# A three-block network on one core: modulation rows move from TensorE to VectorE, MLP units take both halves of x in one matmul, and attention probabilities become the stationary operand

## The chip, the core and the metric

The kernel runs on one core of a Trainium2 chip. Its engines have instruction streams of their own and meet only at semaphores: TensorE (PE in the profile, with its weight loads as PEld), VectorE (DVE), ScalarE (ACT), GpSimd (POOL, which only fills a few constants here) and SyncE (SP), which issues the transfers of the weights. The metric is the time of one execution in microseconds. The median of the runs before is 1037.1 us.

## What is computed

Batch 1, 256 tokens, width 1024, all in 32-bit floats. The reference is a first block of two layers and a second block of one layer:

```python
for i in range(DEPTH):                      # 0: gated delta rule, 1: HGRN
    s = conv_gdn_mixer(...) if i % 2 == 0 else hgrn2_mixer(...)
    x = layer_norm(DEEPNORM_ALPHA * x + s, ln_g[i], ln_b[i])
    gate = sigmoid(x @ w_pl_gate[i])
    x = x + (p[i] @ w_pl[i]) * gate
...
mod = silu(c) @ w_ada[l] + b_ada[l]         # c is one row: 1 x 1024 by 1024 x 6144
sh1, sc1, g1, sh2, sc2, g2 = split(mod[:, None, :], 6, axis=-1)
hn = rms(x, norm1_g) * (1 + sc1) + sh1
y = mixer(hn, w_in, ...)                    # 6 forget-gate heads, 4 mLSTM, 6 block-sparse
x = x + g1 * (y @ w_out)
hn = rms(x, norm2_g) * (1 + sc2) + sh2
gate, up = split(hn @ w_gate_up, 2, axis=-1)
x = x + g2 * ((silu(gate) * up) @ w_down)   # inner width 2816
```

In an attention head, `p = softmax(s)` and the output is `p @ v`; in an mLSTM head the scores are divided by `max(|sum|, exp(-m))` instead.

## The kernel before

**Weights.** All large weights come from HBM as 165 slabs, mostly of 1 MB (128 partitions by 2048 numbers), in a fixed order, into a ring of six buffers `RAW`. SyncE issues the load of slab i when the last user of slab i-6 is done (the function `slab`). A matmul operand `w` or `x` is kept as two parts in the format fp32r: a high part H, rounded, and a low part L, the rest. A product is then three matmuls, H·H, H·L and L·H (`products`). For a weight slab, ScalarE writes the high part `WH` (a ring of three, `s_split`) and VectorE subtracts it from the raw slab, in place, as `WL`. For x the parts are `XTH` and `XTL`, for the input of an output projection `YH` and `YL`.

**Steps and order.** The work is cut into named steps. A step such as `ff:7` has a part on each engine that takes part in it (on "TSV": TensorE, then ScalarE, then VectorE). The order in which each engine runs its steps is written out by hand, in the tables `ORDER_T`, `ORDER_S` and `ORDER_V`; an engine never leaves its order. `split:k:i` is the split of slab i. PSUM has eight banks. Those that a step needs are claimed: TensorE waits until the readers of the previous step in that bank are done. Banks 4 to 7 are a ring for the weight units.

**Modulation rows.** `silu(c)` lies as one column per block of 128 inputs in `SCZ`, padded with zeros to 32 columns. The 6144 outputs are 12 rows of 512; each takes two slabs and two steps, `ada:i:0` and `ada:i:1`. These slabs are not split. A step is four matmuls with a 32-column weight, one per quarter of the partitions of one PSUM bank (`t_ada`). ScalarE copies the bank to `MROW` (`s_ada`), and `adat:i` (`t_adat`, `v_adat`) brings the row where it is used: for eight rows by four transposes and a sum over groups on VectorE, for the four gain rows by a matmul with ones.

**Around them.** The tail of each layer of the first block has the layer norm on VectorE (`lna`, `lnb`), transposes of x (`xt`), and the gate product, whose input the VectorE part of `xt` makes. The rows 0, 1 and 2 stand in the first tail, 3 in the last group of the HGRN layer, 8, 6, 7, 9 and 4 in and behind the second tail, 5 in the attention, 10 and 11 between the output projection (`out2`) and the MLP (`ff`).

**Attention.** For head h: `score` (TensorE; VectorE adds the bias and takes a minimum, ScalarE takes the exponential and the sum), `ratio` (VectorE: reciprocal, then it multiplies the 384 probabilities of each partition by it), `turn` (three transposes, a ScalarE copy to `PTT`), `pv` (three matmuls with v stationary, so that the result is already transposed), and for every second head the split of the result to `YH` and `YL`.

**MLP.** `ff:j`, j from 0 to 21, makes 128 gate and 128 up features in one bank: 16 pairs of a block k and a half a, each with three matmuls of 256 columns. ScalarE takes Silu of the gate half, VectorE multiplies, and splits the result. `down` follows.

Of the kernel before, what the change touches and what calls it, by code (L numbers as in the profile page):

```python
# [115 lines left out]
def plan(stage):  # L116
# [351 lines left out]
    end_row()  # L468
    for j in range(FF):
        unit("ff", j, on="TSV", slab=("ff", j), halves=False)  # L470
# [12 lines left out]
gu:0:3:1 ah:0:1 gx:0:3:1 first:ac:0:1 gp:0:4:1 gp:0:4:0 gx:0:3:0 ac:0:1 gu:0:4:1 gu:0:4:0 first:az:0:1 gx:0:4:0 az:0:1
gp:0:5:1 gp:0:5:0 gx:0:4:1 first:ab:0:1 gu:0:5:0 gu:0:5:1 ab:0:1 gx:0:5:0 gp:0:6:0 gp:0:6:1 gx:0:5:1 first:ah:1:0
gu:0:6:0 gu:0:6:1 ah:1:0 gv:0:0 first:ac:1:0 gs:0 first:az:1:0 gks:0 az:1:0 gv:0:1 ac:1:0 go:0 first:ab:1:0 gr:0:0
ab:1:0 gc:1 first:zb:1:0 zb:1:0 first:zb:1:1 norm:q:1 zb:1:1 first:ah:1:1 ah:1:1 gk:1 vtr:1 first:ac:1:1 gkk:1 ac:1:1
first:ab:1:1 gp:1:0:0 first:az:1:1 gp:1:0:1 gu:1:0:0 az:1:1 ab:1:1 gp:1:1:0 gu:1:0:1 out:0:0:0 gu:1:1:0 gp:1:1:1
# [5 lines left out]
first:gate:0:1:0 first:gate:0:1:1 xt:1:0 gate:0:1:0 gate:0:1:1 adat:1 xt:1:1 ada:2:0 ada:2:1 xt:1:2 xt:1:3 first:f:0:0
first:f:0:1 f:0:1 adat:2 f:0:0 first:q1:0:0 q1:0:0 first:q1:0:1 q1:0:1 first:i:0:0 hd:0 i:0:0 hm:0:0 first:i:0:1
hm:0:1 i:0:1 first:f:1:1 first:f:1:0 hm:0:2 first:z1:0:0 hm:0:3 f:1:0 f:1:1 z1:0:0 first:z1:0:1 z1:0:1 hm:0:4
first:q1:1:0 hm:0:5 q1:1:0 hm:0:6 first:q1:1:1 hc:0 q1:1:1 ho:0 first:i:1:0 hd:1 hr:0:0 i:1:0 first:f:2:0 first:i:1:1
f:2:0 hm:1:0 i:1:1 hm:1:1 first:f:2:1 f:2:1 hm:1:2 first:z1:1:1 first:z1:1:0 hm:1:3 z1:1:0 hm:1:4 first:q1:2:0 z1:1:1
hm:1:5 q1:2:0 hm:1:6 first:q1:2:1 hc:1 q1:2:1 ho:1 first:i:2:0 hd:2 hr:1:0 first:i:2:1 i:2:0 first:f:3:0 f:3:0 hm:2:0
i:2:1 hm:2:1 first:f:3:1 f:3:1 first:z1:2:0 hm:2:2 first:z1:2:1 hm:2:3 z1:2:0 hm:2:4 z1:2:1 hm:2:5 first:q1:3:0 hm:2:6
q1:3:0 hc:2 first:q1:3:1 ho:2 q1:3:1 hr:2:0 hd:3 first:i:3:0 i:3:0 first:i:3:1 hm:3:0 first:z1:3:0 i:3:1 hm:3:1 z1:3:0  # L500
hm:3:2 first:z1:3:1 hm:3:3 z1:3:1 hm:3:4 ada:3:0 ada:3:1 hm:3:5 adat:3 out:1:0:0 hm:3:6 out:1:0:1 hc:3 out:1:1:0 ho:3
out:1:1:1 hr:3:0 out:1:0:2 hr:3:1 pl:1:0 out:1:1:2 first:out:1:0:3 first:out:1:1:3 out:1:0:3 out:1:1:3 pl:1:1 ada:8:0
# [1968 lines left out]
```

## Time and profile before

| | |
|---|---|
| runs | 1037.1 us median of 3 (1036.44 to 1039.84) |
| the profiled execution | 1038.47 us, of which the trace spans 1036.7 |
| TensorE matmul busy | 1016.7 us (98%) |
| TensorE weight load busy | 897.0 us (87%) |
| VectorE busy | 718.1 us (69%) |
| ScalarE busy | 508.8 us (49%) |
| DMA | 181.44 MB, mean 175 GB/s |

All times in a trace are microseconds from the start of the span. Matmuls are pipelined: the duration of one in the trace is longer than its distance to the next, so what one costs in a stream is read from the distance of starts. A wait that a trace names is idle time of the engine before an instruction, with what ended it.

### The profile page before, as it was taken

Reading aid. Unit: us, or ns where it says so; the run is one execution under the profiler, and the core shown is the slowest. Engines: PE = TensorE matmul, PEld = TensorE weight load, DVE = VectorE, ACT = ScalarE, POOL = GpSimd, SP = SyncE. Lnnn points to the kernel's source line nnn. Section 1 sums busy time; section 2 is a strip of 40 time slices with the busy share of each in tenths; the row PEclk is TensorE's granted clock in tenths of the full one; section 3 lists DMA queues with packets and bytes.
Section 4 is the critical chain, followed back from the end, with each engine's and each line's share of the span. In section 5 each row is a group of like instructions: output and inputs, shape, how many; then the busy total and the mean of one; then the engine's idle time right before and its main releaser. Section 6 shows DMA issues by size and latency. Waiting matters only on the chain.

```text
span 1036.7 us, 21071 instructions
## 1 busy us (share of the span) xinstructions
PE 1016.7 (98%) x9120; PEld 897.0 (87%) x9120; DVE 718.1 (69%) x1049; ACT 508.8 (49%) x590; POOL 0.5 (0%) x7
## 2 busy tenths in 40 slices
PE   9999999999999999999999999989998999999998
PEld 7999999999875798989898887669975779999986
DVE  6898946698448656867786856855887775655544
ACT  6764444463253552554555343565767553343331
POOL 0000000000000000000000000000000000000000
PEclk9999999999999999999999999999999999999999
DMA  8454333334227663525343544865523447454541
GB/s 357 164 185 163 123 128 130 135 139 163 83 99 287 258 225 111 202 102 186 123 164 123 188 180 180 341 266 218 201 110 123 152 172 286 162 208 159 192 175 41
DMA packets 26298, 181.44 MB, mean 175 GB/s; under 512 B 3040, under 2 KB 3296, under 8 KB 4960
## 3 DMA queue, kind: packets, MB, share of 16 engines
q1 hardware_dynamic: 25056, 174.66, 45.5%
q10 hardware_dynamic: 1152, 5.45, 1.3%
q8 instruction: 73, 1.20, 0.4%
q14 instruction: 17, 0.14, 0.0%
HBM read 179.04 MB, written 1.05 MB: 174 GB/s over the span
## 4 chain that ended last, share of the span: by engine, by line
PE 91%; DVE 4%; DMA 2%; ACT 2%; issue 1%; POOL 0%; ACTq 0%; POOLq 0%; DVEq 0%
PE PS L916 87%; DMA RAW<-wst 2%; PE PS L1157 1%; PE PS L1079 1%; DVE WL L1814 1%; ACT WH L1386 1%; DVE block L2289 0%; DVE layer_ln L2138 0%; PE PS L1006 0%; DVE block L2274 0%; PE PS L1196 0%; PE PS L1307 0%; ACT block L1694 0%; ACT block L1688 0%; DVE block L2269 0%
## 5 line engine op out<-in xcount | busy, mean ns | idle before, releaser
L1814 DVE TENSOR_TENSOR WL<-RAW,WH 128x2048 fp32r<-128x2048 f32 (+1 forms) x138 | 312.1, 2272 | 137.7 <-ACT WH L1386 137.5
L916 PE MATMUL PS<-XTH,WH 128*128 128x256 f32 x1392 | 404.1, 290 | 0.5 <-issue 0.5
L916 PE MATMUL PS<-XTL,WH 128*128 128x256 f32 x1392 | 394.4, 283 | 0.0
L916 PE MATMUL PS<-XTH,WL 128*128 128x256 f32 x1392 | 394.3, 283 | 0.0
L1386 ACT ACTIVATE WH<-RAW 128x2048 fp32r<-128x2048 f32 x138 | 260.8, 1899 | 236.7 <-PE PS L916 223.9
L916 PEld LDWEIGHTS PS<-XTH,WH 128*128 128x128 f32 x1392 | 267.3, 192 | 4.4 <-issue 2.8
L916 PEld LDWEIGHTS PS<-XTL,WH 128*128 128x128 f32 x1392 | 267.5, 192 | 2.5 <-issue 2.4
L916 PEld LDWEIGHTS PS<-XTH,WL 128*128 128x128 f32 x1392 | 267.4, 192 | 0.0
L916 PE MATMUL PS<-WH,YH 128*128 128x512 f32 x224 | 90.0, 402 | 0.0
L916 PE MATMUL PS<-WH,YL 128*128 128x512 f32 x224 | 87.3, 390 | 0.0
L916 PE MATMUL PS<-WL,YH 128*128 128x512 f32 x224 | 87.2, 389 | 0.0
L916 PE MATMUL PS<-WH,XTH 128*128 128x512 f32 x160 | 65.5, 410 | 2.3 <-ACT MROW L1569 2.1
L916 PE MATMUL PS<-WH,XTL 128*128 128x512 f32 x160 | 62.5, 391 | 0.0
L916 PE MATMUL PS<-WL,XTH 128*128 128x512 f32 x160 | 62.4, 390 | 0.0
L916 PEld LDWEIGHTS PS<-WH,YH 128*128 128x128 f32 x224 | 42.1, 188 | 9.6 <-issue 1.1
L916 PEld LDWEIGHTS PS<-WL,YH 128*128 128x128 f32 x224 | 42.1, 188 | 9.3 <-issue 1.0
L916 PEld LDWEIGHTS PS<-WH,YL 128*128 128x128 f32 x224 | 42.0, 188 | 9.0
L916 PEld LDWEIGHTS PS<-layer 128*32 128x32 f32 (+2 forms) x1920 | 39.2, 119 | 9.0 <-issue 4.2
L1736 ACT ACT_TABLE_LOAD x36 | 46.2, 1283 | 0.6
L916 PE MATMUL PS<-layer 128*32 128x16 f32 (+3 forms) x1920 | 43.9, 198 | 0.9 <-DVE layer L2132 0.8
L916 PEld LDWEIGHTS PS<-WH,XTH 128*128 128x128 f32 x160 | 30.1, 188 | 9.9 <-ACT MROW L1569 2.5
L916 PEld LDWEIGHTS PS<-WH,XTL 128*128 128x128 f32 x160 | 30.0, 188 | 6.6
(293 smaller groups left out, 1082.4 us busy)
## 6 DMA issues: line engine op xcount, KB each, us to landing
RAW<-wst SPq DMA_DIRECT2D x162, 1024.0 KB, 4.9
LNW<-lnrow ACTq DMA_DIRECT2D x3, 1024.0 KB, 7.9
RAW<-wst SPq DMA_DIRECT2D x4, 512.0 KB, 5.7
layer<-xt SPq DMA_DIRECT2D x2, 512.0 KB, 5.3
XR<-x ACTq DMA_DIRECT2D x1, 1024.0 KB, 6.8
out<-X SPq DMA_DIRECT2D x4, 256.0 KB, 2.3
CST<-cst ACTq DMA_DIRECT2D x1, 640.0 KB, 8.7
PT<-pt SPq DMA_DIRECT2D x1, 512.0 KB, 5.5
```

Source lines behind the costliest of these rows:

```text
L916: return pe.matmul(o, lhsT, rhs, start=start, stop=stop)
L1079: last = pe.transpose(PS[:, 2 + c, h * P:(h + 1) * P], U[:, c * HG + h, :], ident)
L1157: last = pe.transpose(PS[:, step.banks[0], o:o + P], src[:, c, k * P:(k + 1) * P], ident)
L1386: fn(WH[:, k % SPLIT_RING, 0:n], RAW[:, i % RAW_RING, 0:n], ACT.Copy).then_inc(scalar_done, 1)
L1736: act.preload_act_table_set(wanted)
L1814: tt(WL[:, i % RAW_RING, 0:n], RAW[:, i % RAW_RING, 0:n], as_float(WH[:, k % SPLIT_RING, 0:n]), ALU.subtract).then_inc(vector_done, 1)
```

## The change

Three edits, and a new order for all engines.

1. `ada:i:0` and `ada:i:1` go to VectorE. `v_ada` multiplies each of the eight blocks of a row by its column of `SCZ` and adds it to `MROW`, with one tensor_scalar and seven scalar_tensor_tensor instructions of 512 elements per row; all 128 partial sums stay apart. `t_adat` then sums over the partitions: for the eight rows by four matmuls with the block of `MROW` stationary and 16 columns of ones moving, for the gain rows as before. `s_ada` is gone. A slab of such a row is free when VectorE is done with it.
2. `XTH` and `XTL` become halves of one tile `XHL`, so that `t_ff` can move 512 columns (both halves) past the high weight, and 256 (the high one) past the low weight: 16 pairs, each with one matmul of 512 and one of 256 columns. A unit now fills two banks, with a part to be added: ScalarE copies one (`fl`), VectorE adds (`fs`), and then the rest follows as before from SBUF. With four banks in the ring, two units fit instead of four.
3. In `pv` the transposed probabilities are stationary (128 columns) and v moves (64 columns). `turn` no longer waits for `ratio`; that only takes the reciprocal. The division comes later, on the output of two heads (`ys`), which is then transposed back by two transposes (`yt`) and split.

```diff
@@ def ada(i): def halves():
-            unit("ada", i, 0, on="T", slab=("ada", i, 0), readers="", halves=False)
-            banks = script[-1].banks
+            step("ada", i, 0, on="V", slab=(("ada", i, 0),), readers="")
             end_row()
-            step("ada", i, 1, on="TS", banks=banks, slab=(("ada", i, 1),), opens=False)
+            step("ada", i, 1, on="V", slab=(("ada", i, 1),), readers="")
@@
-                step("pv", n - 2, on="T", banks=(3,))
...
+            step("pv", n - 2, on="T", banks=(3,), opens=n % 2 == 0)
+            if n % 2:
+                t = (n - 2) // 2
+                step("ys", t, on="V")
+                step("yt", t, on="TS" if FOX // 2 <= t < (FOX + ML) // 2 else "TSV", banks=(3,), opens=False)
@@
-        unit("ff", j, on="TSV", slab=("ff", j), halves=False)
+        step("ff", j, on="TSV", banks=(bank(), bank()), slab=[("ff", j)], readers="V", read_in=("fs", j))
+        step("fl", j, on="S")
+        step("fs", j, on="V")
@@ ORDER_V (one line of each)
-first:out:0:0:3 first:out:0:1:3 lna:0:0 lnb:0:0:0 out:0:0:3 out:0:1:3 lna:0:1 lnb:0:0:1 lnb:0:1:0 lnb:0:1:1 xt:0:0:0
+gr:1:1 ada:0:0 ada:0:1 first:out:0:1:3 first:out:0:0:3 out:0:0:3 lna:0:0 out:0:1:3 lnb:0:0:0 lna:0:1 lnb:0:0:1
@@ t_adat
                 for j in range(4):
-                    last = pe.transpose(PS[:, step.banks[0], j * P:(j + 1) * P], MROW[:, j * P:(j + 1) * P], ident)
+                    last = mm(PS[:, step.banks[0], 16 * j:16 * (j + 1)], row[:, j * P:(j + 1) * P], ONES[:, 0:16],
+                              start=j == 0, stop=j == 3)
@@ t_pv
-                mm(o[:, 0:P], V2[:, 0, vcol:vcol + HD], pt[:, 0:P])
...
+                mm(o[:, 0:HD], pt[:, 0:P], V2[:, 0, vcol:vcol + HD])
+                mm(o[:, HD:P], pt[:, P:2 * P], V2[:, 0, vcol:vcol + HD], stop=False)
+                mm(o[:, HD:P], pt[:, 2 * P:3 * P], V2[:, 1, vcol:vcol + HD], start=False).then_inc(tensor_done, 1)
@@ t_ff
-                features(step, xt_part(5)).then_inc(tensor_done, 1)
+                for k in range(KC):
...
+                    for a in range(2):
+                        s, o = slice(a * P, (a + 1) * P), PS[:, step.banks[a], :]
+                        mm(o, wh[:, k, s], XHL[:, k, :, :].rearrange("p e t -> p (e t)"), start=k == 0, stop=False)
+                        last = mm(o[:, 0:T], wl[:, k, s], XTH[:, k, :], start=False, stop=k == KC - 1)
@@ new on VectorE
+            def v_ada(i, part):
...
+                for j in range(4):
+                    c = SCZ[:, 4 * part + j, 0:1]
+                    if part == 0 and j == 0:
+                        last = ts(row, w[:, j, :], c, None, ALU.mult)
+                    else:
+                        last = stt(row, w[:, j, :], c, row, ALU.mult, ALU.add)
+                    if j < 3:
+                        link(last)
@@ ScalarE and VectorE in the MLP
+                fn(FL[:, j % 2], PS[:, b:b + 2, T:2 * T], ACT.Copy).then_inc(scalar_done, 1)
...
+                tt(FT[:, j % 2], PS[:, b:b + 2, 0:T], FL[:, j % 2], ALU.add).then_inc(vector_done, 1)
```

Where the new order puts the rows is best seen in the built programs. VectorE at the start of the first tail, before the change (X<-XR,PS with BN_STATS is `first:out`, the sum of x and the projection; YL is the end of the mixer):

```order
L1825 CAST YH<-layer_x 128x512
L1826 TENSOR_TENSOR YL<-layer_x,YH 128x512
L1997 SCALAR_TENSOR_TENSOR X<-XR_81,PS 128x512
L1998 BN_STATS STAT<-X 128x6
L1997 SCALAR_TENSOR_TENSOR X<-XR_81,PS 128x512
L1998 BN_STATS STAT<-X 128x6
L2010 BN_AGGR AGG<-STAT 128x2
```

And with the change:

```order
L1851 CAST YH<-layer_x 128x512
L1852 TENSOR_TENSOR YL<-layer_x,YH 128x512
L2102 TENSOR_SCALAR MROW<-RAW,SCZ 128x512
L2104 SCALAR_TENSOR_TENSOR MROW<-RAW,SCZ,MROW 128x512 x7
L2026 SCALAR_TENSOR_TENSOR X<-XR_80,PS 128x512
L2029 BN_STATS STAT<-X 128x6
L2026 SCALAR_TENSOR_TENSOR X<-XR_80,PS 128x512
```

A whole row (`ada:0:0` and `ada:0:1`) now stands between the end of the mixer and the first sum of the layer norm. VectorE between the output projection and the MLP, with the change (L2374 ends `out2`, L2209 to L2213 normalize x, L2070 is `xt:5`, the input of the MLP):

```order
L2374 TENSOR_TENSOR X<-X,block_84 128x512
L2102 TENSOR_SCALAR MROW<-RAW,SCZ 128x512
L2104 SCALAR_TENSOR_TENSOR MROW<-RAW,SCZ,MROW 128x512 x3
L2209 SCALAR_TENSOR_TENSOR SUMSQ<-SUMSQ,SUMA 128x1
...
L2213 TENSOR_SCALAR block_84<-X,RSTD 128x1024
L2104 SCALAR_TENSOR_TENSOR MROW<-RAW,SCZ,MROW 128x512 x4
L2070 TENSOR_SCALAR PS<-PS,MODG,MODT 128x256 x2
L2075 TENSOR_TENSOR XHL<-PS,XHL 128x2x256
```

Before, no instruction of a modulation row stood on VectorE here; both halves of row 11 now lie around the normalization. In the same way rows 6, 7 and 9 lie between the gate products of the second tail.

## Rows read from the trace of the kernel before

**Rows 1.** The page: busy us (share of the span) and instructions.

```profile
PE 1016.7 (98%) x9120; PEld 897.0 (87%) x9120; DVE 718.1 (69%) x1049; ACT 508.8 (49%) x590; POOL 0.5 (0%) x7
```

**Rows 2.** Windows: stretch, length, busy PE, PEld, DVE, ACT, POOL, clock, DMA.

```profile
336.80:341.34 4.54, 4.54 (x21) 3.75 (x20) 2.45 (x4) 3.29 (x4) 0.00 (x0) 1.00 1.00 413
314.90:366.20 51.30, 49.96 (x268) 36.67 (x267) 37.84 (x57) 25.73 (x32) 0.00 (x0) 1.00 0.71 265
561.90:603.20 41.30, 40.87 (x650) 33.81 (x649) 36.59 (x44) 19.43 (x15) 0.00 (x0) 1.00 0.55 198
623.90:698.40 74.50, 69.82 (x360) 49.94 (x359) 50.67 (x83) 37.39 (x56) 0.00 (x0) 0.98 0.69 267
759.00:820.20 61.20, 56.31 (x350) 39.96 (x349) 47.33 (x168) 41.13 (x101) 0.00 (x0) 1.00 0.37 138
820.20:848.30 28.10, 27.50 (x151) 19.68 (x151) 20.92 (x32) 16.78 (x29) 0.00 (x0) 1.00 0.40 150
848.30:971.00 122.70, 122.70 (x1025) 122.70 (x1024) 70.89 (x83) 45.46 (x42) 0.00 (x0) 1.00 0.53 198
```

**Rows 3.** TensorE's groups: shapes, count, busy us, mean ns, idle before.

```profile
L916 PE MATMUL PS<-RAW,SCZ 128*32 128x512 f32 x192 | 23.3, 598 | 4.0 <-DMA RAW<-wst 4.0
...
L916 PE MATMUL PS<-block,values 128*64 128x128 f32 x96 | 9.3, 281 | 0.0
...
L1307 PE MATMUL PS<-CST,block 128*128 128x128 f32 x48 | 8.3, 282 | 4.6 <-DVE block L2289 3.2 <-ACT block L1702 1.4
...
L916 PE MATMUL PS<-WBA,layer 128*128 128x16 f32 x32 | 3.6, 260 | 0.0
```

**Rows 4.** Timeline of TensorE: start us, us, what, count, idle before.

```profile
330.86 2.78 PE L916 MATMUL PS<-RAW,SCZ 128*32 128x512 f32 x24
333.57 0.66 PE L1157 MATMUL PS<-CST,X 128*128 128x128 f32 x4
...
688.43 1.06 PE L916 MATMUL PS<-RAW,SCZ 128*32 128x512 f32 x8 [3.48 <-DMA RAW<-wst]
```

**Rows 5.** The chain that ended last, a piece of transposes.

```profile
353.00 0.44 PE PS L1157 x4
```

**Rows 6.** Timeline of TensorE in `ff`.

```profile
870.83 0.28 PE L916 MATMUL PS<-XTH,WH 128*128 128x256 f32 x1
870.95 0.28 PE L916 MATMUL PS<-XTL,WH 128*128 128x256 f32 x1
```

**Rows 7.** VectorE's groups by shape: count, busy us, mean ns, idle before.

```profile
L1814 DVE TENSOR_TENSOR WL<-RAW,WH 128x2048 fp32r<-128x2048 f32 x136 | 309.7, 2287 | 131.4 <-ACT WH L1386 131.3
...
L2044 DVE TENSOR_TENSOR XTL<-PS,XTH 128x512 fp32r<-128x512 f32 x12 | 8.0, 684 | 1.2 <-ACT XTH L1543 1.0
...
L2020 DVE SCALAR_TENSOR_TENSOR X<-X,AGG,LNW 128x512 f32<-128x512 f32 x8 | 6.0, 748 | 0.4 <-DMA LNW<-lnrow 0.2
...
L2289 DVE TENSOR_SCALAR block<-block 128x256 f32<-128x256 f32 x16 | 5.6, 347 | 0.0
...
L2289 DVE TENSOR_SCALAR block<-block 128x128 f32<-128x128 f32 x16 | 4.6, 287 | 0.6
```

**Rows 8.** Timeline of VectorE: first sum, two linked instructions, one of 1024 elements.

```profile
316.82 0.69 DVE L1997 SCALAR_TENSOR_TENSOR X<-XR,PS 128x512 f32<-128x512 f32 x1 [1.92 <-PE PS L916]
...
327.05 0.74 DVE L2020 SCALAR_TENSOR_TENSOR X<-X,AGG,LNW 128x512 f32<-128x512 f32 x1
327.82 0.75 DVE L2021 SCALAR_TENSOR_TENSOR X<-X,RSTD,LNW 128x512 f32<-128x512 f32 x1
...
839.08 0.75 DVE L2162 TENSOR_SCALAR block<-X,RSTD 128x1024 f32<-128x1024 f32 x1
```

**Rows 9.** ScalarE's groups in `ff`, 848.3 to 971.

```profile
L1386 ACT ACTIVATE WH<-RAW 128x2048 fp32r<-128x2048 f32 x21 | 39.8, 1909 | 17.5 <-PE PS L916 16.9 <-DMA RAW<-wst 0.6
L1722 ACT ACTIVATE mlp<-PS 128x256 f32<-128x256 f32 x20 | 7.3, 380 | 51.6 <-PE PS L916 41.0 <-DVE YL L2332 10.6
```

**Rows 10.** Timeline of TensorE at the start of the MLP.

```profile
844.88 0.68 PE L916 MATMUL PS<-XTH,WH 128*128 128x256 f32 x1
```

More of the change, by code:

```diff
@@ L468, in plan @@
     end_row()
+    while ring[0] % 2:
+        bank()
     for j in range(FF):
[L470 removed]
+        step("ff", j, on="TSV", banks=(bank(), bank()), slab=[("ff", j)], readers="V", read_in=("fs", j))
+        step("fl", j, on="S")
+        step("fs", j, on="V")
     for n in range(2):
@@ L483 @@
[L483 to L487, printed above, removed]
@@ L493 @@
[L493 to L497, printed above, removed]
@@ L498 @@
[L498 to L502, printed above, removed]
@@ L516 @@
+pv:11 turn:13 score:15 score:14 yt:5 out2:0:0 pv:12 pv:13 turn:14 yt:6 turn:15 adat:5 pv:14 pv:15 yt:7 out2:1:0
+first:out2:0:1 out2:0:1 first:out2:1:1 out2:1:1 adat:10 xt:5:1 xt:5:0 adat:11 xt:5:3 xt:5:2 ff:0 ff:1 ff:2 ff:3 ff:4
+ff:5 ff:6 ff:7 ff:8 ff:9 ff:10 ff:11 ff:12 ff:13 ff:14 ff:15 ff:16 ff:17 ff:18 ff:19 ff:20 ff:21 down:0:0 down:0:1
+down:0:2 down:0:3 down:0:4 down:1:0 first:down:0:5 down:0:5 down:1:1 down:1:2 down:1:3 down:1:4 first:down:1:5
+down:1:5
 """
 ORDER_S = """
-setup split_top xs:1 split:0:0 xs:0 split:1:1 ba1 split:2:2 ba2 c1 split:3:3 k:0:0 split:4:4 k:0:1 norm:k:0 v:0:0
@@ new lines @@
+split:43:48 lb first:gate:0:0:1 gate:0:0:1 split:44:51 xtl:1:1 xtl:1:0 first:gate:0:1:1 split:45:52 gate:0:1:1
+split:46:53 xtl:1:2 adat:1 xtl:1:3 ada:2:0 ada:2:1 split:47:54 adat:2 lb2 f:0:0 f:0:1 split:48:55 split:50:57 hd:0
+split:49:56 hy:0:0 hp:0:0 hy:0:1 split:51:58 hy:0:2 split:53:60 split:52:59 hy:0:3 hp:0:1 split:54:61 f:1:0 hy:0:4
+hp:0:3 hp:0:2 hy:0:5 hp:0:4 hy:0:6 split:55:62 hp:0:6 hy:0:7 f:1:1 split:57:64 hp:0:5 split:56:63 hz:0 hy:1:0 hd:1
+split:58:65 hr:0:0 split:59:66 hy:1:1 hp:1:1 hy:1:2 split:60:67 hp:1:0 f:2:0 hp:1:2 hy:1:3 split:62:69 hy:1:4 hy:1:5
@@ new lines @@
+hr:3:0 hr:3:1 ada:8:0 split:82:91 mod:0 split:83:92 wg2 ada:8:1 first:out:1:0:3 first:out:1:1:3 lna:1:0 lnb:1:0:0
+out:1:0:3 out:1:1:3 lna:1:1 lnb:1:0:1 lnb:1:1:0 xt:2:0:0 lnb:1:1:1 split:84:98 xt:2:0:1 split:85:99 xt:2:1:0 ada:6:0
+xt:2:1:1 ada:6:1 adat:8 split:86:100 first:gate:1:0:1 ada:7:0 split:87:101 gate:1:0:1 ada:7:1 first:gate:1:1:1
+split:88:105 gate:1:1:1 ada:9:0 rmsb:0:0 rmsb:0:1 ada:9:1 xt:4:1 xt:4:3 xtl:4:0 xtl:4:1 xtl:4:2 ada:4:0 xtl:4:3 adat:6
+split:89:109 adat:7 ada:4:1 adat:9 split:90:110 gates:0 gates:1 ga split:91:111 split:92:112 gb qn:1:2 split:93:113
@@ L864, in rows @@
             return slice(0, P) if c == 0 else slice(P, 3 * P)
-        ada_rows = [s.args[0] for s in script if s.kind == "ada" and s.args[1] == 0]
+        ada_rows = [s.args[0] for s in order["V"] if s.kind == "ada" and s.args[1] == 0]
         x_users = [(k, 1, p) for k in ("k", "v", "q", "zb", "ah", "ac", "az", "ab") for p in range(2)]
@@ L1996, in add_out @@
                 x = X[:, c, s]
-                link(stt(x, XR0[:, c, s] if layer == 0 else x, ALPHA, PS[:, bank_of("out", layer, n, 3) + c, :], ALU.mult, ALU.add))
+                product = PS[:, bank_of("out", layer, n, 3) + c, :]
+                if layer == 0:
+                    k = 4 * c + 2 * n
+                    link(stt(two(x), XR0[:, k:k + 2, :], ALPHA, two(product), ALU.mult, ALU.add))
+                else:
+                    link(stt(x, x, ALPHA, product, ALU.mult, ALU.add))
                 return dve.bn_stats(STAT[:, c, n, :], x)
```

353 lines of the change are left out of this document (192 added, 161 removed).

## The prediction

> **What bounds the kernel now.** I read the page's busy shares first. TensorE is busy for 98% of the span, VectorE for 69% and ScalarE for 49% [rows 1], so that over the whole kernel TensorE is the bound. An average hides stretches with another limit, so I read the windows next, cut at the places where the change puts its new VectorE work [rows 2]. The column to look at is the fourth figure, VectorE's busy time, against the length. In the MLP VectorE has 70.9 us of work in 122.7: free half of the time, while TensorE runs without a gap. In the end of the HGRN layer (561.9 to 603.2) it has 36.6 of 41.3, in the first tail 37.8 of 51.3, in the second tail, from the end of the last mixer group to the input of the second block, 50.7 of 74.5, and between attention and MLP 20.9 of 28.1. These last are the four stretches in which the modulation rows are made. They are also those where TensorE waits on what VectorE makes: the input of the gate product and of the MLP.
>
> **The rows, what TensorE gives up.** Three steps `ada` take from 330.86 to 333.57, when the next instruction starts: 0.90 us each [rows 4]. There are 24 of them: 21.6 us, close to the 23.3 us of their group [rows 3]. `adat` for eight rows was four transposes at 0.11 us each, 0.44 us [rows 5]; now it is four matmuls of two passes with a full 128-column weight and 16 columns moving, a shape that the trace has: 32 passes in 3.6 us, 0.1125 each [rows 3]. That is 0.90 us for a row, 0.46 more, 3.7 us for eight. Net 17.9 us of TensorE work less. One of these steps had waited 3.48 us for its slab [rows 4].
>
> **The rows, what VectorE takes on.** A scalar_tensor_tensor of 512 elements from SBUF takes 748 ns [rows 7], and with the link to the next 0.77 to 0.79 us from start to start (327.05 to 327.82) [rows 8]: 0.78. The one tensor_scalar lies between 347 ns at 256 elements [rows 7] and 0.75 us at 1024 [rows 8], on a line 0.48, with its link 0.52. A row costs 0.52 + 7 x 0.78 = 5.98 us, twelve rows 71.8 us. The kernel could hide them in the MLP's free half, but they are needed before it, and stand where I have just counted. Stretch by stretch, VectorE's work then and the length now:
>
> - First tail: 37.8 + 2 rows (12.0) = 49.8 us for 51.3. It just fits, if VectorE never waits. But the layer norm goes through ScalarE and back twice, and `ada:0:0` and `ada:0:1` come ahead of the first sum, for which VectorE waits 1.92 us [rows 8]; the sum moves back by several us. The gain on the other side is that the slabs of the gate product are asked for earlier. I take +0.8 us, and -4 (TensorE's four steps at 0.9, if all is hidden) to +4 as bounds.
> - HGRN end: 36.6 + 6.0 = 42.6 us for 41.3: +1.2, bounds -1.3 (1.8 saved less 0.46) and +4.
> - Second tail: rows 8, 6, 7 and 9 whole and the first half of row 4 (0.52 + 3 x 0.78 = 2.9) are 26.8 us: 50.7 + 26.8 = 77.5 for 74.5, +3.0. With the two round trips through ScalarE and the waits for the first results, about 1.4 more: +4.4. Bounds: -10 (ten steps of 0.9, and part of the 3.48 us wait, less `adat`) and +8.
> - Between attention and MLP: rows 10 and 11 are 12.0 us: 20.9 + 12.0 = 32.9 for 28.1, +4.8. The halves of row 11 lie around the normalization and so straight on the way to the first `ff`, at 844.88 in the trace [rows 10]. Bounds -2 and +7.
>
> Together +11.2 us where TensorE loses 17.9 us of work. What was cover for these steps is gone: before, TensorE's own 0.9 us steps ran while VectorE normalized.
>
> **The MLP.** A matmul of 256 columns comes every 0.12 us (870.83, 870.95) [rows 6]. Of 512 columns, the row 336.80:341.34 of [rows 2] has 21 in 4.54 us of the gate product, the first of them begun before it: 20 starts, one every 0.227 us. A pair cost 3 x 0.12 = 0.36 and costs 0.227 + 0.12 = 0.347 us; 22 x 16 pairs give 352 x 0.013 = 4.6 us less, 4.4 with the last digit's rounding (0.0125 each). The Trainium skill ("TensorE: Matmul & The Clock Gate", Back-to-back issue gap) gives N/2.4 + 2.5 ns for one matmul alone, by which two of 256 columns take 218.3 ns against 215.8 for one of 512, and the edit would be worth 352 x 2.5 ns = 0.9 us, an estimate from that page. The rows show about 13 ns over the columns' own time at both sizes, and they decide. The new copies are hidden: per unit of 5.56 us ScalarE has 1.91 for the split, 0.38 for Silu [rows 9] and at most 0.76 for the copy of 512, twice Silu's 256; VectorE has 2.29 for the split, 0.68 for the sum (as L2044, [rows 7]) and its present (70.9 - 22 x 2.29) / 22 = 0.93, or more: 1.2 for three full instructions. So about 3 and 4.2 of 5.56. I take -4.4; bounds -4.4 and +20 (third rival).
>
> **Attention.** The weight of `pv` grows from 64 to 128 columns and the moving side shrinks from 128 to 64. Before, 96 passes took 9.3 us [rows 3]; now 96 at 0.1125 are 10.8, and 16 transposes back at 0.11 add 1.8. Row 5 leaves TensorE (1.8 less). So its work grows by 1.5 us. VectorE loses 16 x (0.287 + 0.347) = 10.1 us [rows 7], gains eight products of 256 at about 0.42 (between 347 ns for 256 elements with one operand and 684 for 512 with two [rows 7]) and one row: 47.3 - 10.1 + 3.4 + 6.0 = 46.6 of 61.2 [rows 2]. The chain of one head gets shorter by the reciprocal and two products, and TensorE waited 4.6 us before `turn` [rows 3]. But bank 3 must be read, divided, transposed and read again before the next pair may start, and one half of row 5 stands in front of `score:13`. I take -2: half of the wait and some gaps win 5, less 1.5 of work and 1.5 of new waits. Bounds -7 and +5.
>
> **The sum.** 0.8 + 1.2 + 4.4 + 4.8 - 4.4 - 2.0 = +4.8 us. The profiled execution took 1038.47 (span 1036.7), so 1043.3 for one like it; it is 1.4 above the median, and against 1037.1 it is 1041.9. I predict 1042 us.
>
> **Rivals.** (A) TensorE stays the bound everywhere: for it speak 98% busy [rows 1]. Then all of its work counts: -17.9 for the rows, -4.4 for `ff`, and attention's own additions 1.5 + 1.8 = 3.3, since row 5 is already in the 17.9: -19.0, 1018 us. Against it, the windows: in two stretches VectorE would have more work than time. That is also where the Trainium skill points ("Perfetto Trace Analysis", Identifying the Most-Contended Engine): optimize the engine of the highest occupancy first. Read over the span, that rule gives this rival; its next section says that the most contended engine can change over time, and the rows say that it does.
>
> (B) The rows fall into VectorE's idle time and cost nothing in the tails, since TensorE's transposes and slabs come earlier there and the new order starts work sooner, but give nothing either; attention gives its full 6: -4.4 - 6 = -10, 1027, with 1024 to 1034 around it. For it: VectorE's 1.92 us before the first sum [rows 8], and 13 and 24 us free in the two tails [rows 2].
>
> (C) The MLP starves. With two units in four banks, unit j+2 waits for `fs:j`. If a split stands ahead on both engines, that is 1.9 + 0.6 + 2.3 + 0.7 = 5.5 us after the unit's end, against 5.56 us of the one unit in between. It decides from a delay of 0.1 us on; at 0.5 to 1 us for each of 22 units it costs 11 to 22, less the 4.4 that I had: 1055 to 1065.
>
> (D) Cost and gain cancel: half of the +11.2 in the tails, and the rest as above: 1034 to 1040.
>
> **Chances.** My forecast 0.50, its own range 1037 to 1048; A 0.10; B 0.22; C 0.08; D 0.10. A difference of 0.3% is about what a measurement of this kernel can tell from none: 1034.0 to 1040.2. Faster: A and most of B, 0.30. Same: D, a little of B, and 0.08 of the forecast: 0.20. Slower: the rest of the forecast and C, 0.50. The range leaves out A and C: 1025 to 1049.
>
> **What would show it.** A row on VectorE should be 5.9 to 6.0 us, VectorE's busy total 718 + 72 + 15 (22 sums) - 7 = about 798. The first `ff` should start 8 to 12 us later than 844.88, the end of the second tail at its latest link on VectorE, with TensorE waiting for XHL and WL in the tails; `ff` itself should run at 5.56 us a unit with no gaps. I am wrong if TensorE's idle time in the tails stays as it was (then A or B), or if a scalar_tensor_tensor on `RAW` takes well under 0.75 us; and on the other side if TensorE waits for VectorE at each unit of the MLP (C).

## The result and the profile after

The changed kernel takes 1055.3 us (median of 3, 1055.21 to 1055.48) where the kernel before takes 1037.1: ratio 1.0166, 95% interval 1.0152 to 1.0181. The forecast was 1042 in a range to 1049: the sign was right, the size is nearly four times too small (18.2 us against 4.8).

The page's rows of the changed kernel, beside [rows 1], and of its granted clock by slices:

```profile
PE 1010.5 (96%) x8624; PEld 893.5 (85%) x8624; DVE 790.8 (75%) x1135; ACT 519.5 (49%) x603; POOL 0.5 (0%) x7
...
PEclk8999999999998999999999999979999889999999
```

Three numbers tell the story before any wait is looked at. The span grew by 17.0 us (1036.7 to 1053.7), but TensorE is busy for 6.2 us less. So its idle time grew by 23.2 us, from 20.0 to 43.2. And by my own sums TensorE's work fell by 17.9 for the rows and 4.4 for the units, and grew by 3.3 in attention: 19.0 less. Busy fell by 6.2 only, so by this account, an estimate that rests on those sums, some 12.8 us of what is shown as busy is the same work done slower: the mean granted clock is 0.977 where it was 0.997. VectorE has 790.8 us, 798 was expected: its costs were priced rightly.

From TensorE's timelines, the time between the same steps (us):

| stretch | before | changed | difference | my forecast |
|---|---|---|---|---|
| start to last `out` of layer 0 | 324.6 | 325.7 | +1.1 | 0 |
| first tail, to the first `f` | 37.9 | 39.1 | +1.2 | +0.8 |
| HGRN, to its last `out` | 285.2 | 290.5 | +5.3 | +1.2 |
| second tail, to `feat:8` | 47.2 | 50.6 | +3.4 | +4.4 |
| `feat:8` to the last `out2` | 141.6 | 145.7 | +4.1 | -2.0 |
| last `out2` to first `ff` | 8.5 | 14.1 | +5.6 | +4.8 |
| first `ff` to first `down` | 127.1 | 123.4 | -3.7 | -4.4 |

Two of these rows have to be read with care. The +1.1 of the first row is no effect of the change: up to that step, TensorE takes 324.1 to 325.7 us in the traces with the new order (E3, E4, E7, E10, E14) and 324.6 to 325.5 in those with the old one (before, E1, E2, E5, E6, E9, E13). And my +1.2 for the HGRN layer was the forecast for its end alone. Up to `hd:3`, the start of the last group, the layer is 3.0 us longer, for which I had nothing; behind `hd:3` it is 2.3 us longer.

The windows that answer to the last six stretches of [rows 2]:

```profile
316.00:368.60 52.60, 46.93 (x222) 37.53 (x221) 47.56 (x68) 22.97 (x26) 0.00 (x0) 0.94 0.69 258
567.20:609.70 42.50, 40.45 (x633) 34.42 (x632) 36.41 (x42) 19.07 (x14) 0.00 (x0) 0.96 0.49 182
628.50:709.40 80.90, 66.36 (x296) 52.67 (x295) 73.43 (x113) 36.29 (x53) 0.00 (x0) 0.92 0.66 252
768.60:835.30 66.70, 63.26 (x361) 49.47 (x360) 49.77 (x156) 43.92 (x102) 0.00 (x0) 0.95 0.36 127
835.30:869.00 33.70, 26.24 (x113) 20.74 (x113) 31.37 (x49) 13.18 (x25) 0.00 (x0) 0.85 0.34 125
869.00:988.00 119.00, 119.00 (x682) 104.00 (x681) 83.14 (x101) 59.04 (x64) 0.00 (x0) 1.00 0.58 212
```

The figure to see is the granted clock, the third from the end: it was 0.98 to 1.00 in all six before, and is 0.85 to 0.96 in five of them now. What happens there is seen in the end of the second tail. TensorE's timeline, where [rows 4] has its steps `ada`:

```profile
689.78 0.96 PE L929 MATMUL PS<-ONES,MROW 128*128 128x16 f32 x8
699.49 3.65 PE L1170 MATMUL PS<-CST,block 128*128 128x128 f32 x16 [8.76 <-DVE block L2213]
702.93 1.73 PE L929 MATMUL PS<-ONES,MROW 128*128 128x16 f32 x8
705.82 0.77 PE L929 MATMUL PS<-XHL,WH 128*128 128x256 f32 x2 [1.16 <-DVE XHL L2075]
```

and the windows before the wait, in it, and behind it:

```profile
677.80:689.90 12.10, 12.09 (x58) 10.08 (x59) 11.43 (x15) 4.77 (x5) 0.00 (x0) 1.00 0.89 354
689.90:699.40 9.50, 0.84 (x9) 0.74 (x7) 9.08 (x19) 4.89 (x13) 0.00 (x0) 0.78 0.89 349
699.50:705.80 6.30, 5.16 (x24) 5.06 (x25) 5.38 (x10) 4.26 (x8) 0.00 (x0) 0.50 0.73 303
705.80:712.90 7.10, 7.08 (x48) 7.10 (x49) 6.99 (x11) 1.58 (x2) 0.00 (x0) 0.79 0.00 0
```

Where TensorE had five row steps and a wait of 3.48 us before, it now stands idle for 8.76 us. In the 6.3 us behind the wait the granted clock is 0.50, the lower of its two levels (1.2 of 2.4 GHz): the same 8-pass sum over partitions takes 1.73 us at 702.93 that took 0.96 at 689.78. The wait is on VectorE, and its timeline shows a half row, 2.8 us of the 8.76, in the chain to the instruction that ends it (L2102 and L2104 are the row, L2213 is what TensorE waits for):

```profile
693.02 0.69 DVE L2083 TENSOR_TENSOR X<-X,norms 128x512 f32<-128x512 f32 x1
693.63 0.48 DVE L2102 TENSOR_SCALAR MROW<-RAW,SCZ 128x512 f32<-128x512 f32 x1
694.15 2.33 DVE L2104 SCALAR_TENSOR_TENSOR MROW<-RAW,SCZ,MROW 128x512 f32<-128x512 f32 x3
...
698.59 0.75 DVE L2213 TENSOR_SCALAR block<-X,RSTD 128x1024 f32<-128x1024 f32 x1
```

The end of the HGRN layer has the same picture in small. The second half of row 3 stands ahead of what VectorE makes for the steps `hm` of the last group, and TensorE then waits for VectorE three times:

```profile
586.09 3.11 DVE L2104 SCALAR_TENSOR_TENSOR MROW<-RAW,SCZ,MROW 128x512 f32<-128x512 f32 x4
```
```profile
592.14 0.73 PE L929 MATMUL PS<-layer 128*32 128x16 f32 x64 [0.77 <-DVE layer_ln L2189]
596.40 0.85 PE L929 MATMUL PS<-layer 128*32 128x16 f32 x64 [0.47 <-DVE layer L2183]
598.99 1.54 PE L929 MATMUL PS<-layer 128*64 128x64 f32 x32 [0.74 <-DVE layer L2183]
```

In attention, where I had forecast a gain, the steps take the same time as in a kernel with the new attention and rows on TensorE (E6) from the end of `feat:8` up to `turn:11`, within 0.2 us; then comes one wait of 1.46 us for ScalarE, and the lower clock for 6.6 us:

```profile
816.01 0.88 PE L929 MATMUL PS<-values,block 128*128 128x64 f32 x6
818.34 0.87 PE L1315 MATMUL PS<-CST,block 128*128 128x128 f32 x3 [1.46 <-ACT block L1711]
```
```profile
818.30:824.90 6.60, 6.56 (x27) 5.21 (x28) 4.56 (x14) 4.69 (x9) 0.00 (x0) 0.51 0.25 104
824.90:829.50 4.60, 4.60 (x23) 3.79 (x22) 4.56 (x10) 2.79 (x9) 0.00 (x0) 1.00 0.45 137
```

On VectorE a half of row 5 lies beside this wait (812.9 to 815.7), but it isn't what TensorE waits for. With that half row cut from 2.8 to 1.2 us (E3) the wait at the same step is 1.45 us. E12 has row 5 on TensorE, but moved away from here, and a wait of 1.35 us; E6 has row 5's two steps on TensorE at just this place (802.4 to 804.2), and no wait. So the wait stands where the row's own TensorE steps had been cover. First E3, then E12:

```profile
815.53 0.52 PE L1315 MATMUL PS<-CST,block 128*128 128x128 f32 x3 [1.45 <-ACT block L1711]
```
```profile
805.13 0.87 PE L926 MATMUL PS<-block,values 128*64 128x128 f32 x6 [1.35 <-ACT block L1721]
```

Not each wait brings the lower clock. Windows of the changed kernel behind the waits before the gate product of the first tail (0.8, 1.8 and 3.0 us), behind two of 2.12 and 1.57 us in the second tail, and behind 6.33 us before the MLP:

```profile
338.00:344.00 6.00, 5.98 (x17) 4.73 (x18) 5.82 (x7) 0.00 (x0) 0.00 (x0) 0.54 0.30 127
658.80:677.00 18.20, 14.32 (x73) 11.43 (x71) 17.78 (x25) 10.54 (x11) 0.00 (x0) 1.00 0.69 258
859.00:866.00 7.00, 5.79 (x20) 4.27 (x21) 6.51 (x12) 2.25 (x5) 0.00 (x0) 0.51 0.01 2
```

The Trainium skill ("TensorE: Matmul & The Clock Gate", section "HAM oscillation — how this bites in real kernels") tells of a kernel whose waits for data let the clock fall, so that what follows each of them starts at half speed. This trace agrees for the waits of 8.76 and 6.33 us. It has the same behind a wait of 1.46 us too, with one of 0.84 us shortly before it, and nothing of it behind those of 2.12 and 1.57 us.

### The profile page after: what moved, and what is told of

Its sections match the earlier page's. It is cut to its first block, busy times and chain, and to the rows that moved or that the text cites. A ratio compares the mean times of both kernels' runs of the same rounds, so it can differ in the third digit from the quotient of the medians.

```text
span 1053.7 us, 20208 instructions
## 1 busy us (share of the span) xinstructions
PE 1010.5 (96%) x8624; PEld 893.5 (85%) x8624; DVE 790.8 (75%) x1135; ACT 519.5 (49%) x603; POOL 0.5 (0%) x7
## 4 chain that ended last, share of the span: by engine, by line
PE 86%; DVE 10%; issue 2%; ACT 1%; DMA 1%; SPq 0%; DVEq 0%; ACTq 0%
PE PS L929 83%; DVE WL L1840 2%; DVE MROW L2104 1%; PE PS L1092 1%; PE PS L1170 1%; DMA RAW<-wst 1%; DVE layer_ln L2189 1%; PE PS L1315 1%; DVE X L2051 1%; DVE layer L2182 0%; DVE layer L2181 0%; PE PS L1019 0%; DVE X L2052 0%; PE PS L1331 0%; DVE STAT L2029 0%
## 5 line engine op out<-in xcount | busy, mean ns | idle before, releaser
L929 PE MATMUL PS<-XHL,WH 128*128 128x256 f32 (+1 forms) x2432 | 513.8, 304 | 3.2 <-DVE XHL L2075 1.2
L929 PEld LDWEIGHTS PS<-XHL,WH 128*128 128x128 f32 x2432 | 393.8, 193 | 24.6 <-issue 4.9
L929 PE MATMUL PS<-XHL,WL 128*128 128x256 f32 x1392 | 394.5, 283 | 0.0
L1840 DVE TENSOR_TENSOR WL<-RAW,WH 128x2048 fp32r<-128x2048 f32 x138 | 312.7, 2270 | 81.5 <-ACT WH L1410 81.5
L929 PEld LDWEIGHTS PS<-XHL,WL 128*128 128x128 f32 x1392 | 267.5, 192 | 0.0
L929 PE MATMUL PS<-WH,XHL 128*128 128x512 f32 x320 | 107.6, 405 | 4.8 <-DVE XHL L2060 3.0
L929 PEld LDWEIGHTS PS<-WH,XHL 128*128 128x128 f32 x320 | 61.2, 191 | 18.9 <-DVE XHL L2060 3.2
L2104 DVE SCALAR_TENSOR_TENSOR MROW<-RAW,SCZ,MROW 128x512 f32<-128x512 f32 x84 | 63.0, 750 | 2.8
L929 PE MATMUL PS<-WL,XHL 128*128 128x512 f32 x160 | 63.3, 396 | 0.0
L929 PEld LDWEIGHTS PS<-WL,XHL 128*128 128x128 f32 x160 | 30.7, 192 | 6.3 <-issue 0.7
```

Of the source, the lines that this page charges most:

```text
L929: return pe.matmul(o, lhsT, rhs, start=start, stop=stop)
L1840: tt(WL[:, i % RAW_RING, 0:n], RAW[:, i % RAW_RING, 0:n], as_float(WH[:, k % SPLIT_RING, 0:n]), ALU.subtract).then_inc(vector_done, 1)
L2104: last = stt(row, w[:, j, :], c, row, ALU.mult, ALU.add)
```

## The experiments

Sixteen kernels ran. All ratios are against the kernel before, run beside them.

**E1 and E2: undo the rows; the units alone.** E1 is the changed kernel with the rows back on TensorE in the order of before; E2 is before with the new units.

```diff
-            step("ada", i, 0, on="V", slab=(("ada", i, 0),), readers="")
+            unit("ada", i, 0, on="T", slab=("ada", i, 0), readers="", halves=False)
```

> The changed kernel with one part undone: the modulation rows are back on TensorE (steps, ScalarE copy, transposes and their places in the order as before), the new attention and the new MLP units stay. Theory R (the 18.2 us are lost because the rows stand on VectorE where TensorE waits for it): about 1037 - 3.7 for the MLP units + 0 to 2 for attention = 1033 to 1036 us. Rival P (the attention edit costs about 5 us by itself): 1038 to 1040. If the rows are not the cause: above 1048.

> The kernel before with the MLP units' edit alone (both halves of x side by side, one matmul of 512 columns, two banks a unit). In the changed kernel the stretch from first to last matmul of the units is 3.7 us shorter, so theory R says 1033 to 1034 us. A rival, that the copies and sums push other work of VectorE or the start of the down products: 1036 to 1038.

Measured: 1.0080 (1.0061 to 1.0099) and 1.0035 (1.0024 to 1.0046), both outside every expectation. The cause was mine, in E1 too, which has this wait and one of 3.1 us before the MLP. E2's trace is that of before up to the first unit, and then, on TensorE:

```profile
854.88 0.76 PE L926 MATMUL PS<-XHL,WH 128*128 128x512 f32 x1 [4.25 <-DVE LNW L2095]
```
```profile
854.80:859.30 4.50, 4.42 (x14) 3.77 (x15) 0.00 (x0) 0.00 (x0) 0.00 (x0) 0.50 0.54 224
```

The second unit needs the bank from which VectorE reads row 11's sums, and I had put that read behind the first unit's sum. Without having sought it, this measures a wait by itself: 4.25 us idle, then 14 matmuls in 4.5 us where the mended kernel has 27 in as long.

**E5 and E6: the same two, mended.**

```diff
-xtl:5:2 xtl:5:3 split:106:130 fs:0 split:107:133 adat:11 fs:1
+xtl:5:2 xtl:5:3 adat:11 split:106:130 fs:0 split:107:133 fs:1
```

> The run of the MLP units alone gave 1.0035 where 0.996 was expected; its trace is that of before up to the first unit (within 0.4 us), then the second unit waits 4.5 us, since its bank is that of row 11's transposes and my order had VectorE read them behind the first unit's sum; some 4 us of matmuls at half clock follow. Here that read stands ahead of the first splits and sums, nothing else changes. If that explains the miss: 4.5 + 2.5 us less, 1034 to 1035 against a before of 1038, ratio 0.995 to 0.997. If the units cost elsewhere: 1.000 or above.

> The rows on TensorE as before, the new attention and the new MLP units. The first run of this had the 4.5 us wait in the MLP, and one of 3.1 us before the MLP, where ScalarE's copy of row 10 stood behind a split (order of my own); both places now have the order of before. In the first run out2 began 0.6 to 1.0 us from where it does before. Theory R: attention is worth -1 to +1 us, ratio 0.995 to 0.998. Rival P (probabilities stationary costs some 5 us): 1.000 to 1.003.

Measured: 0.9961 (0.9949 to 0.9973), and 0.9979 (0.9969 to 0.9988). The units alone are worth 4.0 us (2.8 to 5.3), and E5 is the fastest kernel of this case, with E12 level. In E5's trace only 2.3 us of it lie in the units (124.8 us for 127.1), and 2.0 in the second tail, where the clock doesn't fall this time (1.00 from 684 to 694 us, with a wait of 3.2 us in it); in E6 and in the changed kernel the units' stretch is 4.0 and 3.7 us shorter. The new attention costs some 2 us by the two ratios (0.3 to 3.4), though the two profiled spans are the same, 1032.3 and 1032.4; its stretch is 0.7 us longer. TensorE's idle time there falls from 4.9 to 2.3 us, and the transposes and longer passes take its place. The whole loss of the changed kernel, 1.87% over E6, lies in the rows and in the order made for them.

**E3: short rows.** Order, waits and counts are kept; VectorE's total falls from 790.8 to 752.0 us.

```diff
+                if at or part:
+                    row, w = MROW[:, 0:64], w[:, :, 0:64]
```

> The changed kernel with its order, waits, slabs and instruction counts as they are, but all row instructions after the first half row work on 64 of the 512 columns (the other columns of the modulation are left out), so that VectorE spends about 22 us on them and not 71. Theory R: the time of the instructions is the cost: 13 to 18 us come back, 1037 to 1042 us. Rival W (it is not their length but their place: the waits for slabs, the order, the release of the slabs by VectorE): less than 5 us come back, 1050 to 1055.

Measured: 1.0088 (1.0061 to 1.0116): 8 us of 17 come back, 5 to 11 with the intervals. Between both theories: the length of the instructions is about half of the loss. By stretches it is very uneven. The end of the HGRN layer is back at 84.9 us (84.8 before, 87.1 changed), and the stretch before the MLP falls from 14.1 to 11.7. The second tail stays at 50.5: its longest wait is 6.9 us for 8.8, but the clock falls once more (0.59 from 658 to 666 us, where the changed kernel has 1.00).

**E4: filled waits.**

```diff
+WARM = {('xt', 0, 1, 0): 2, ('first', 'gate', 0, 0, 0): 3, ('xt', 4, 0): 10, ('xt', 5, 1): 7}
...
+                for _ in range(WARM.get(step.name, 0)):
+                    mm(PS[:, step.banks[0], :], ONES[:], ONES[:].unsqueeze(1).to_broadcast([P, 4, P]))
```

> The changed kernel with filler matmuls (constants into the bank that is written next, 0.86 us each) in TensorE's longest waits: 2 and 3 before the gate product of the first tail (waits of 1.8 and 3.0 us), 10 before the transposes of the second block (9.5 us) and 7 before those of the MLP (6.3 us). Theory C (after such a wait the granted clock is at half for some 6 us, and that is on the path): no dip of the clock at 338, 699 and 859 us, and 5 to 8 us less, 1047 to 1050. Rival (VectorE's chain ends these stretches anyway, the slow clock lies beside it): 1053 to 1056.

Measured: 1.0121 (1.0096 to 1.0145), 4.7 us less than the changed kernel by the ratios (1.7 to 7.4); the median, 1052.0, lies between both expectations. The mean clock is 0.987 to 0.993 where it was 0.977. Work that computes nothing makes the kernel faster. The dips at 338 and 859 us are gone and that at 699 is shorter (from 703 on); a new one stands in the HGRN layer (0.59 from 478 to 482), behind a wait of 1.73 us. The window of the last transposes before the MLP, where the changed kernel has 0.71 from 860 to 870 us:

```profile
858.30:863.00 4.70, 4.70 (x30) 4.00 (x29) 4.70 (x9) 4.06 (x6) 0.00 (x0) 1.00 0.00 0
```

**E14: both.** Short rows, and E4's fillers with two more.

> The changed kernel with short row instructions (64 columns, 1.0088 alone) and filler matmuls in TensorE's waits (1.0121 alone, against 1.0166 for the changed kernel), and one filler each in two more waits (before turn:12 and hm:3:5). If instruction length and half clock are two causes that add up: 1.0166 - 0.0078 - 0.0045 = 1.004, and 1.001 to 1.003 with the two further fillers. If short rows have already taken the waits away in which the clock falls: 1.007 to 1.009.

Measured: 1.0084 (1.0064 to 1.0105), in the second range and the same as E3 (1.0088). It doesn't tell which theory holds: with short rows the waits are shorter than the fillers, and the stretch before the gate product grew from 6.6 us (E3) to 9.1, that before `xt:4` from 8.1 to 9.7. How the two causes share the loss stays open.

**E9 and E13: does TensorE's row work hold anything up?** Both take it from the kernel before and add nothing.

```diff
-                for j in range(4):
+                for j in range(1):                                       # E9
```
```diff
-                    last = mm(PS[32 * j:32 * (j + 1), step.banks[0], :], SCZ[:, 4 * part + j, :], w[:, j, :],
+                    last = mm(PS[32 * j:32 * (j + 1), step.banks[0], 0:64], SCZ[:, 4 * part + j, :], w[:, j, 0:64],   # E13
```

> The kernel before with three of four matmuls left out in each of the 24 row steps on TensorE (three quarters of each modulation sum are missing); nothing is added anywhere. TensorE has 24 x 0.9 x 3/4 = 16.2 us less to do. Rival A (TensorE, 98% busy, is the bound everywhere): 16 us less, ratio 0.984. Theory K (in the tails these steps only fill stretches whose end VectorE, ScalarE and the slabs' DMA set; removed there, nothing comes back, and TensorE then stands idle and may lose its clock): only the four steps of rows 3 and 5 and a few of the others count, 3 to 7 us less, ratio 0.993 to 0.997.

> The kernel before with each of the row steps' matmuls on 64 of the 512 columns (seven eighths of each modulation row are missing). A step of 0.90 us becomes some 0.11 to 0.2, so TensorE has 24 x 0.7 to 0.79 = 17 to 19 us less to do, and nothing is added. Rival A (TensorE is the bound everywhere): ratio 0.982 to 0.984. Theory K (in the tails and before the MLP these steps fill stretches that others end): only rows 3 and 5 and part of the others count, 3 to 7 us less, ratio 0.993 to 0.997; TensorE's idle time grows by the rest.

E9 measured 1.0000 (0.9990 to 1.0010), and says nothing on the question: the edit took no time away. TensorE's group, beside that of [rows 3]:

```profile
L916 PE MATMUL PS<-RAW,SCZ 128*32 128x512 f32 x48 | 23.0, 598 | 3.5 <-DMA RAW<-wst 3.5
```

48 matmuls in 23.0 us, 192 in 23.3: the four of a step write to four quarters of the partitions, and run side by side. E13 takes the time away, and measured 0.9999 (0.9989 to 1.0008). Each of the 24 steps is 0.6 to 0.75 us shorter, TensorE is busy for 13.5 us less (1003.2), and the span is that of before within 0.1 us. Where it went, in the second tail, first before, then E13:

```profile
652.96 2.78 PE L916 MATMUL PS<-RAW,SCZ 128*32 128x512 f32 x24
655.78 1.07 PE L1157 MATMUL PS<-CST,X 128*128 128x128 f32 x8
```
```profile
652.30 0.54 PE L916 MATMUL PS<-RAW,SCZ 128*32 128x64 f32 x24
655.83 1.46 PE L1157 MATMUL PS<-CST,X 128*128 128x128 f32 x8 [2.98 <-DVE X L2021]
```

The transposes start at 655.8 in both. Of the 18 us cut, 13.5 came back as idle time: by who ended the waits, some 8 for VectorE, 4 for slabs and 2 for ScalarE. (E13's mean clock was 0.989, 0.57 and 0.51 in new or longer dips at 656 and 687 us, so the other 4.5 are shown busy still, by an estimate from these sums: the same work at the lower clock.) This is the central result: an engine that is 98% busy, and 18 us of its work are worth nothing, since they stand where it would wait; and where the waits were longer, a part of what followed them ran slower. Not even Theory K's 3 to 7 us came. Rows 3 and 5 gave back all they saved, at waits of 1.43 us for VectorE and 0.99 for ScalarE: the end of the HGRN layer takes 84.9 us (84.8 before), the attention 141.6 (141.6). Rival A is refuted.

**E7, E8, E15: better places.** E7: the changed kernel, rows 10 and 11 inside the MLP. E8: the order of before, all rows on VectorE in steps of one instruction, in its idle times. E15: E5, with rows 3 and 5 alone moved so.

```diff
-    ada(10)[0]()
     quarters(5)
-    ada(11)[0]()
...
+        if j in MLP_ADA:
+            i, part = MLP_ADA[j]
+            step("ada", i, part, on="V", slab=(("ada", i, part),), readers="")
```

> The changed kernel with rows 10 and 11 moved out of the way to the MLP into it, into VectorE's free half (halves behind the sums of units 3, 6, 10 and 13, their sums on TensorE two units later, in banks 0 and 1); only the down products need them. The stretch from the last out2 matmul to the first unit is 14.05 us in the changed kernel, 8.46 before. Theory R (place is the cost): it falls to 8 to 10 us and the clock's dip at 859 us goes with it, the units stay at 123.4 plus 1.7 for two sums: 4 to 7 us less than the changed kernel, ratio 1.010 to 1.013. Rival C (the MLP starves when VectorE has more): each half row delays a unit by 1 to 3 us and eats the gain, ratio 1.016 or more.

> The order of before (attention as before too) with the new MLP units, and all twelve rows on VectorE, but each in eight steps of one instruction, put where VectorE is idle by the trace of before: row 0 in the wait of 7.4 us at 289, 1 at 372, 2 at 415, 3 at 447, 8 at 506 and 523, 6 at 557, 7 at 615, 9 at 626 and 640, 4 at 707 and 717, 5 at 731 to 799, 10 and 11 in the MLP. TensorE has 17.9 us less in rows and 3.7 to 4.4 less in the units. Theory R: most of it comes out, ratio 0.983 to 0.990 (1018 to 1026 us by this before). Rival: the rows cost wherever they stand, since slabs are held longer and VectorE's chains are delayed: 1.000 or above.

> The kernel before with the new MLP units (0.9961) and only rows 3 and 5 on VectorE, in steps of one instruction, in its waits of 9.5 us at 606 and of 5.6 and 3.0 us at 709 and 726, with their slabs asked for just before; all other rows stay on TensorE as cover. TensorE loses four steps of 0.90 us in stretches that it fills, and gains 0.46 for row 3. Theory: 3.1 us less, ratio 0.993. Rival (the slabs are held longer or VectorE's queue is late): 0.996 or above.

Measured: 1.0214 (1.0197 to 1.0231), 1.0662 (1.0644 to 1.0680), 1.0027 (1.0014 to 1.0040): all three slower than their base (the changed kernel, E5, E5), and all in the range of the rival: my place theory falls. Three things were missing from it. First, in E7 a half row of 2.85 us stands ahead of a split for which TensorE waits (its waits in the MLP; in the changed kernel they were 0.2 us):

```profile
PE PS L931 <- DVE WL L1842: 3.7, 2, 2.5
```

and the MLP took 130.8 us where 125.1 were due: rival C, which the changed kernel escapes. And the stretch before the MLP is 11.7 us though no row stands there, where it is 8.5 in the kernel before: TensorE waits 6.8 us idle, and its transposes run at the lower clock. Second, a slab is held until VectorE has used it, and those behind it come late. E8's waits from 300 to 700 us (the first of them was 8.1 us in the kernel before):

```profile
ACT WH L1440 <- DMA RAW<-wst: 35.4, 8, 14.2
...
DVE MROW L2125 <- DMA RAW<-wst: 12.4, 2, 7.8
...
PE PS L969 <- DVE MODT L2142: 9.1, 1, 9.1
```

Third, E15: with its steps gone TensorE reaches the next product of the HGRN layer early, and waits there for VectorE:

```profile
590.45 0.73 PE L958 MATMUL PS<-layer 128*32 128x16 f32 x64
592.93 1.15 PE L958 MATMUL PS<-layer 128*64 128x64 f32 x32 [1.75 <-DVE layer L2223]
```

The two steps of row 3 (1.8 us) came back as this wait of 1.75; row 5's slabs cost another 2.3 at `feat:3` (a wait of 2.1), and its missing cover a wait of 1.35 at `pv:10`. With E5 as base, the HGRN layer, the second tail and the attention are 1.6, 1.6 and 3.9 us longer; the 1.6 of the second tail are the dip of the clock that E5's trace doesn't have.

**E10, E11, E16: order against rows.** E10: the new order, rows on TensorE. E11: the old order, half rows on VectorE where the changed kernel has them. E16: E11 with short rows.

> The changed kernel with its own order of all other work, the rows back on TensorE at the places that they have before. Against the run with the same parts in the order of before (ratio 0.998) it tells what the new order costs by itself. In the changed kernel the stretch from first f to first hm is 1.4 us longer, the HGRN layer 1.5 to 3 us, and the last sums of out2 by tokens come in an order that has the first 128 tokens ready some 2 us later. Theory O (the order carries a good part of the loss): ratio 1.003 to 1.008. Rival (it is the rows alone): 0.996 to 1.000.

> The order of before, new attention and MLP units, and the rows on VectorE as half rows at the places that they have in the changed kernel. Fourth corner of the square with the changed kernel (1.0166), the rows on TensorE in the order of before (0.998) and in the new one. Theory R with K: most of the loss is here too, ratio 1.010 to 1.018. If the new order is the cause: 0.998 to 1.004.

> The old order with half rows on VectorE (1.0535) and the row instructions on 64 columns: 50 us less for VectorE. If the instructions' length is the cause: 20 to 40 us come back, ratio 1.015 to 1.035. If it is what they wait for in this order (the one row buffer, whose sum over partitions stands behind other steps of TensorE, and the slab queue behind them): less than 10 us, 1.044 or above.

| | rows on TensorE | rows on VectorE | short |
|---|---|---|---|
| old order | 0.9979 (E6) | 1.0535 (E11) | 1.0334 (E16) |
| new order | 1.0195 (E10) | 1.0166 (changed) | 1.0088 (E3) |

Each interval is within 0.003. E10 and E11 came out above both of their expectations; E16, with 21 us back, is in the range for the instructions' length. Neither order is cheap or dear by itself: each fits the rows that it was made for. In the old order the rows cost 5.6%, and the new order takes two thirds of that back. My hand put the rows in E10 and E11 (in E10 TensorE waits 4.2 us for ScalarE's copies of rows, in E11 VectorE 10.4 us for the one row buffer), so I take both as upper bounds.

**E12: two moves in TensorE's order** on E5.

```diff
-adat:6 ada:7:0 ada:7:1 ada:9:0 ada:9:1 ada:4:0 adat:7 xt:4:0 xt:4:1 xt:4:2 adat:9 ada:4:1 xt:4:3
+adat:6 ada:7:0 ada:7:1 ada:9:0 ada:9:1 adat:7 xt:4:0 xt:4:1 xt:4:2 adat:9 xt:4:3 ada:4:0 ada:4:1
```

> Before with the new MLP units (0.996) and two moves in TensorE's order alone: row 4's steps, whose slab TensorE waits 3.2 us for with the transposes of the second block behind it, go behind those transposes; row 5's steps go from behind mln into waits of 0.7 and 1.4 us in attention. VectorE's input for the transposes is ready at about 687 us in that trace, and they start at 689.6. Theory: 2 to 2.5 us from the first, 1 to 1.8 from the second, ratio 0.992 to 0.993. Rival (the waits only move, the slab comes no earlier): 0.995 to 0.997.

Measured: 0.9965 (0.9953 to 0.9978), no better than E5: the rival's range. `xt:4` starts 2.3 us earlier, and the two steps of row 4 now stand where nothing waits, and cost their 1.8. The second move made the attention 1.5 us longer (143.1 for 141.6): where row 5's steps had stood, TensorE waits 1.35 us.

## Why the prediction was wrong

- **Where the sum is short.** It gave +4.8 and the stretches give +17.0, 12.2 more. Of these 6.1 are in attention and 4.1 in the HGRN layer; layer 0's 1.1 is chance, and the other four stretches are 0.9 together.
- **The first failed step is the attention term, -2.0**, measured +4.1. It let "half of the wait and some gaps win 5", and counted row 5's steps as 1.8 us less to do. E6 has the edit with the rows on TensorE: the idle time fell by 2.5 us, and the stretch grew by 0.7. E13 took most of row 5's 1.8 us away and the stretch stayed the same, 141.6: they were cover. In the changed kernel a wait of 1.46 us stands in their place, and the lower clock behind it for 6.6 us; 1.3 us more are `feat:8` at the lower clock, behind the wait of the second tail.
- **The second is that cover was named and not priced.** I had seen that "what was cover for these steps is gone", and wrote its price as VectorE's surplus of work over length alone, and only where the rows stand. In the HGRN end that gave +1.2, measured +2.3: half a row stood ahead of what TensorE needed, and three waits of 2.0 us together and some 3 us at half clock followed (0.57 from 599 to 603 us). E13 gives the other half of it: that time, all 18 us of it, was worth nothing.
- **No term of the sum had the clock.** In the changed kernel it fell behind five groups of waits, and in four of them 5 to 10 us of TensorE's work ran at half clock (in the HGRN end 3.4): 12.8 us of the busy time by the account above, 4.7 us of the kernel's time by E4.
- **The new order** I priced at nothing. It has the 3.0 us ahead of `hd:3`: two transposes of the tail and the longer `adat:2` moved in there (1.25 us together), and two waits of 0.8 and 1.1 us (473 and 479 us). E3 has them too (2.8 us), with its rows short.
- **Right, and in part by luck**: both tails (+1.2 and +3.4 for +0.8 and +4.4) and the stretch before the MLP (+5.6 for +4.8). In each of them 5 to 6 us of TensorE's work ran at half clock, of which the sum knew nothing, and in E4's trace, which has less of that, they are 1.5, 1.0 and 1.7 us shorter. So the surplus was put too high by something like this, and the two errors met. The first `ff` came 20.7 us later than 844.88, and not 8 to 12.
- **Right**: VectorE's durations (790.8 for 798), the units (-3.7 in the stretch, 4.0 us alone, for -4.4; the gap of the Trainium skill, "TensorE: Matmul & The Clock Gate", Back-to-back issue gap, would have given 0.9), and that they don't starve. A and B fell; C was real from the moment that VectorE had a half row more in the MLP (E7).

What stays open is how the loss shares between length, clock and order: E3 and E4 give 8 and 4.7 us, but E14 failed to join them.

## What to carry to other kernels

Before you move work off the busiest engine, ask at each place what that engine would do instead: if it would wait there, the work was free, and moving it saves nothing and adds to the other engine. Test it first by making the work thin where it stands (E13 is one line, and would have told that there was nothing to win). And price a wait on TensorE with what may follow it at half clock: 6.6 us of work at half clock lose about 3.3, so the hole of 1.5 us cost nearly 5, an estimate from these numbers; a filler of useless matmuls can win some of that back.
